# Other memory for the first ring slots, later loads of four heads' query weights, and 64x64 blocks for every weighted row

## The reference

```python
q = (ub @ wq).reshape(tb, PEER_HEADS, 2, PEER_DKEY // 2)
s1 = jnp.einsum('thd,hnd->thn', q[:, :, 0], sub_keys[:, 0])
s2 = jnp.einsum('thd,hnd->thn', q[:, :, 1], sub_keys[:, 1])
t1, i1 = lax.top_k(s1, PEER_TOPK)
t2, i2 = lax.top_k(s2, PEER_TOPK)
...
g = jax.nn.softmax(top.astype(jnp.float32), axis=-1)
act = jax.nn.gelu(jnp.einsum('td,tkd->tk', ub, up[eidx]))
return jnp.einsum('tk,tkd->td', g * act, down[eidx])
```

## Time and profile before

| | |
|---|---|
| median of 3 runs | 4134.78 us (4134.16 to 4145.85) |
| profiled execution, its own time | 4144.19 us |
| span of that execution (first to last instruction) | 4142.4 us |
| PE (TensorE matmul) busy | 3560.7 us, 86% |
| VectorE (DVE) busy | 2749.1 us, 66% |
| ScalarE (ACT) busy | 1717.3 us, 41% |
| GpSimd (POOL) busy | 1877.7 us, 45% |
| DMA queue of the gathers, share of 16 engines | 81.4% |
| mean granted clock of TensorE | 0.980 |

### The profile page before, as it was taken

How to read it: one execution, slowest core, us unless ns; L and a number is a source line. 1 busy time by engine, 2 the same in 40 slices (tenths; PEclk the granted TensorE clock), 3 DMA queues, 4 the chain that set the end, 5 groups by cost and what they waited for, 6 DMA issues and landing times.

```text
span 4142.4 us, 46906 instructions
## 1 busy us (share of the span) xinstructions
PE 3560.7 (86%) x12376; PEld 1549.9 (37%) x12376; DVE 2749.1 (66%) x6907; ACT 1717.3 (41%) x4832; POOL 1877.7 (45%) x1449
## 2 busy tenths in 40 slices
PE   6999999888888888887788877889988888888887
PEld 3445654433333333333211111665433333333332
DVE  3205677777767677777766765668767777767775
ACT  2013625444444444444444443454444444444443
POOL 1112116556556556554434432213545655655555
PEclk9998999999999999999999998999999999999999
DMA  7742349999999999999999998547999999999997
GB/s 278 243 174 57 130 186 416 421 421 421 420 419 415 415 420 416 415 418 416 416 418 409 412 415 322 146 183 293 421 421 421 421 419 416 420 413 415 414 421 331
DMA packets 244603, 1496.45 MB, mean 361 GB/s; under 512 B 25665, under 2 KB 44609, under 8 KB 73649
## 3 DMA queue, kind: packets, MB, share of 16 engines
q0 software_dynamic: 191232, 1385.58, 81.4%
q1 hardware_dynamic: 53168, 108.50, 7.6%
HBM read 1487.57 MB, written 2.21 MB: 360 GB/s over the span
## 4 chain that ended last, share of the span: by engine, by line
DMA 45%; PE 27%; issue 8%; DVE 7%; ACT 6%; POOL 5%; POOLq 0%; DVEq 0%; SPq 0%; ACTq 0%; PEldq 0%
DMA arena<-in_updown,arena 43%; PE psum L1197 8%; POOL arena L1798 4%; DVE arena L2312 4%; PE psum L1140 3%; PE psum L988 3%; PE psum L1004 2%; ACT arena L1585 1%; PE psum L1012 1%; PE psum L1167 1%; ACT arena L1581 1%; PE psum L1273 1%; ACT L1634 1%; ACT L1570 1%; PE psum L1095 1%
## 5 line engine op out<-in xcount | busy, mean ns | idle before, releaser
L1798 POOL DMA_INDIRECT arena<-in_updown,arena x1280 | 1755.4, 1371 | 1739.2 <-PE psum L1197 822.4
L1197 PE MATMUL psum<-arena 128*128 128x512 f32 x4096 | 1992.2, 615 | 340.5 <-ACT arena L1585 323.3
L2312 DVE CUSTOM_DVE_ANT_0 arena<-arena 128x1024 bf16<-128x1024 f32 x1276 | 1565.3, 1227 | 902.1 <-DMA arena<-in_updown,arena 795.9
L1197 PEld LDWEIGHTS psum<-arena 128*128 128x128 f32 x4096 | 710.7, 190 | 1393.9 <-ACT arena L1585 835.2
L1634 ACT ACTIVATE arena<-arena 128x1 f32<-128x1 f32 x1280 | 259.1, 202 | 1665.8 <-DVE arena L2312 1662.8
L1585 ACT ACTIVATE arena<-CN,arena 128x128 f32<-128x128 f32 x1280 | 513.9, 402 | 44.8
L1273 PE MATMUL psum<-arena 64*64 64x512 f32 x2048 | 290.4, 639 | 137.2 <-ACT arena L1585 137.0
L1581 ACT ACTIVATE arena<-arena 128x1 f32<-128x1 f32 x1280 | 376.7, 294 | 67.2 <-ACT arena L1634 4.3
L1167 PE MATMUL psum<-arena 128*128 128x256 f32 (+1 forms) x1280 | 363.1, 384 | 3.0 <-ACT arena L1556 1.6
L1167 PEld LDWEIGHTS psum<-arena 128*128 128x128 f32 x1280 | 239.0, 190 | 260.1 <-issue 252.3
L1273 PEld LDWEIGHTS psum<-arena 64*64 64x64 f32 x2048 | 54.5, 135 | 327.4 <-ACT arena L1585 313.2
(11 more groups left out here) (236 smaller groups left out, 2689.5 us busy)
## 6 DMA issues: line engine op xcount, KB each, us to landing
arena<-in_ada_w POOLq DMA_DIRECT2D x40, 1024.0 KB, 5.9
arena<-in_updown,arena POOLq DMA_INDIRECT x1280, 14.7
arena<-in_wq SPq DMA_DIRECT2D x16, 1024.0 KB, 18.9
arena<-in_w_in SPq DMA_DIRECT2D x50, 256.0 KB, 7.3
arena<-in_w_in SPq DMA_DIRECT2D x5, 2048.0 KB, 14.5
arena<-in_w_in SPq DMA_DIRECT2D x17, 512.0 KB, 4.8
arena<-in_ada_w SPq DMA_DIRECT2D x4, 2048.0 KB, 14.5
arena<-in_bias SPq DMA_DIRECT2D x16, 512.0 KB, 5.9
```

Source lines behind the costliest of these rows:

```text
L1197: mm = e.matmul(ps[ACCUMULATORS[t % 2][hf]][:], diag[:, k % DIAGS, :], ring[k % RING][:, D + hf * 512:D + (hf + 1) * 512], start=first, st ...
L1798: e.indirect_dma_start(ring[k % RING], None, updown, bass.IndirectOffsetOnAxis(ap=idx16[:, k:k + 1], axis=0)).then_inc(sem(f"rows{k % RING ...
L2312: e.tensor_tensor_reduce(prod[:, k % 2, :], ring[k % RING][:, 0:D], u, 1.0, 0.0, ALU.mult, ALU.add, dots[:, k:k + 1]).then_inc(sem("expert ...
```

## The change

It has three parts.

1. The first four gathers of each layer go to `early_ring`, the parts of `wk` that belong to heads 4 to 7, and wait for nothing but their indices. The ring's order is turned: slots 0 to 3 are now the four in `wo`, used from k = 8 on, and slots 4 to 6 the three in `mixT`.
2. The query weights of heads 4 to 7 may not be loaded before those four rows have been weighed: SP waits for `slot_done` 4 ahead of `load_head(4)`. The row `g2r`, issued behind the heads on the same queue, comes after them.
3. `weigh` has the body of `weigh_quarters` everywhere, and ScalarE always reads the swapped half with two instructions of 64 partitions.

```diff
-        ring = ([Region(mixer_top + n * 2 * D)(2 * D) for n in range(MIX_SLOTS)] + [Region(wo_at + n * 2 * D)(2 * D) for n in range(WO_SLOTS)]
+        ring = ([Region(wo_at + n * 2 * D)(2 * D) for n in range(WO_SLOTS)] + [Region(mixer_top + n * 2 * D)(2 * D) for n in range(MIX_SLOTS)]
                 + [last_slot])
+        LATE_HEADS = PH - WO_SLOTS
+        early_ring = [wk[:, 2 * (LATE_HEADS + n):2 * (LATE_HEADS + n) + 2].rearrange("p c k n -> p (c k n)") for n in range(WO_SLOTS)]
+
+        def slot_rows(n, k):
+
+            return early_ring[k] if isinstance(n, int) and n + k < WO_SLOTS else ring[k % RING]
...
                 for h in range(1, PH):
+                    if h == LATE_HEADS:
+                        e.wait_ge(sem("experts.slot_done"), WO_SLOTS)
                     load_head(h)
...
                     for hf in range(2):
-                        mm = e.matmul(ps[ACCUMULATORS[t % 2][hf]][:], diag[:, k % DIAGS, :], ring[k % RING][:, D + hf * 512:D + (hf + 1) * 512],
-                                      start=first, stop=last, skip_group_check=True)
+                        for i in range(2):
+                            rows, o = slice(64 * i, 64 * i + 64), 64 * (i ^ hf)
+                            mm = e.matmul(ps[ACCUMULATORS[t % 2][hf]][o:o + 64, :], diag[rows, k % DIAGS, rows],
+                                          rows_at[rows, D + hf * 512:D + (hf + 1) * 512], start=first, stop=last, skip_group_check=True)
...
-                    if k < MIX_SLOTS:
-                        turned = min(2 * (k + 1) - t0, nt)
+                    if WO_SLOTS <= k < WO_SLOTS + MIX_SLOTS:
+                        turned = min(2 * (k - WO_SLOTS + 1) - t0, nt)
                         if turned > 0:
                             e.wait_ge(sem("experts.y_ready"), turned)
-                    if k == MIX_SLOTS:
-                        e.wait_ge(sem("experts.y_ready"), nt)
                     if k == RING - 1:
                         e.wait_ge(sem("experts.ln1_done"), 1)
+                    if k == RING:
+                        e.wait_ge(sem("experts.y_ready"), nt)
```

More of the change, by code:

```diff
@@ L1195, in weigh @@
                     e.wait_ge(sem("experts.diag_ready"), n + (k + 1))
+                    if not isinstance(n, int):
+                        e.sem_inc(sem("pe_token"), 1)
+                    rows_at = slot_rows(n, k)
                     for hf in range(2):
-                        mm = e.matmul(ps[ACCUMULATORS[t % 2][hf]][:], diag[:, k % DIAGS, :], ring[k % RING][:, D + hf * 512:D + (hf + 1) * 512],
-                                      start=first, stop=last, skip_group_check=True)
+                        for i in range(2):
+                            rows, o = slice(64 * i, 64 * i + 64), 64 * (i ^ hf)
+                            mm = e.matmul(ps[ACCUMULATORS[t % 2][hf]][o:o + 64, :], diag[rows, k % DIAGS, rows],
+                                          rows_at[rows, D + hf * 512:D + (hf + 1) * 512], start=first, stop=last, skip_group_check=True)
                     mm.then_inc(sem("experts.slot_done"), 1)
@@ L1265, in section_mm @@
                         mm.then_inc(sem("ahead.slice_mm"), 1)
[L1267 to L1275, removed]
                 def ahead_unit(t, h):
@@ L1288, in ahead_unit @@
                             section_mm(x, y, a)
-                        (weigh_quarters if t >= CTX_AT else weigh)(t, un * TOPK, k, h == 0 and k == 0, h == PH - 1 and k == TOPK - 1)
+                        weigh(t, un * TOPK, k, h == 0 and k == 0, h == PH - 1 and k == TOPK - 1)
                 def folding_unit(h, turn=None):
@@ L1695, in tile @@
                     e.activation(ysb[:, 0:512], sums[0][:], ACT.Copy)
[L1696 to L1700, removed]
+                    e.activation(ysb[0:64, 512:D], sums[1][64:P, :], ACT.Copy)
+                    ins = e.activation(ysb[64:P, 512:D], sums[1][0:64, :], ACT.Copy)
                     ins.then_inc(sem("experts.acc_free"), 1)
@@ L1795, in _, with gather @@
                 meet(e, "pool")
-                def gather(k):
-                    e.indirect_dma_start(ring[k % RING], None, updown,
+                def gather(k, rows):
+                    e.indirect_dma_start(rows, None, updown,
                                          bass.IndirectOffsetOnAxis(ap=idx16[:, k:k + 1], axis=0)).then_inc(sem(f"rows{k % RING}"), 16)
@@ L1802, in _ @@
                         e.wait_ge(sem("experts.idx_ready"), k // RING + 1)
-                    if k < MIX_SLOTS:
-                        turned = min(2 * (k + 1) - t0, nt)
+                    if WO_SLOTS <= k < WO_SLOTS + MIX_SLOTS:
+                        turned = min(2 * (k - WO_SLOTS + 1) - t0, nt)
                         if turned > 0:
                             e.wait_ge(sem("experts.y_ready"), turned)
-                    if k == MIX_SLOTS:
-                        e.wait_ge(sem("experts.y_ready"), nt)
                     if k == RING - 1:
                         e.wait_ge(sem("experts.ln1_done"), 1)
+                    if k == RING:
+                        e.wait_ge(sem("experts.y_ready"), nt)
                     if k >= RING:
                         e.wait_ge(sem("experts.slot_done"), k + 1 - RING)
-                    gather(k)
+                    gather(k, slot_rows(0, k))
                 with e.Fori(1, nt * PH) as un:
@@ L1820, in _ @@
                         e.sem_inc(sem("pool_token"), 1)
-                        gather(k)
+                        gather(k, ring[k % RING])
         @block.vector
@@ L2311, in dot @@
                         e.wait_ge(sem("experts.dot_done"), un * TOPK + (k - 1))
-                        e.tensor_tensor_reduce(prod[:, k % 2, :], ring[k % RING][:, 0:D], u, 1.0, 0.0, ALU.mult, ALU.add, dots[:, k:k + 1]).then_inc(sem("experts.dot_done"), 1)
+                        e.tensor_tensor_reduce(prod[:, k % 2, :], slot_rows(un * TOPK, k)[:, 0:D], u, 1.0, 0.0, ALU.mult, ALU.add, dots[:, k:k + 1]).then_inc(sem("experts.dot_done"), 1)
                     def opening_unit():
```

2 lines of the change are left out of this document (1 added, 1 removed).

## The result

Over 16 runs each, the changed kernel takes 4154.7 us (median; 4147.3 to 4163.2) and the kernel before 4140.4 us (4131.2 to 4145.9): a ratio of 1.0039, 95% interval 1.0029 to 1.0049, or some 16 us (0.0039 x 4140; the interval is 12 to 20 us). The two medians themselves differ by 14.3 us. The profiled execution took 4158.8 us with a span of 4157.0, against a span of 4142.4 before: 14.6 us more.

What follows compares the result with a forecast made beforehand. The prediction took DMA transfers, at 421 GB/s in both expert stages, as the bound. Layer 0 (10.0 - 2.5), layer 1 (10.0 - 2.0) and the tail 0.5 summed to +16.0 us on 4134.8, giving 4150.8, range 4130 to 4162.

Steps and rivals of the forecast that it cites:

- The ceiling, 421 GB/s: In both expert stages transfers set the pace, at most 421 GB/s over long stretches, so one gather costs 2.49 us.
- Part 1, early gathers: Each layer's opening: four more gathers move early, 10.0 us of transfer, mostly spent as idle time before the eleventh gather.
- The eleventh gather 2.2 us sooner through quarters: Each opening: quarters shorten the chain to the third weighed row by 2.2 us, so this gather goes out at 611.5 and 2848.1.
- The stretch behind it stays full: After the eleventh gather until about 660 us in layer 0, likewise layer 1: losses avoided, gaining 2.5 and 2.0 us.
- Part 2, 10.0 us a layer: Query weights of heads 4 to 7, 4.19 MB, issued around 613 when the engines are full, cost 10.0 us per layer.
- Part 3 in the full stretches, nothing: Quarters in the full-size stretches: worth at most 14.6 us, taken as nothing because the DMA share is 1.01 in both.
- The tail, +0.5: After the last row, the second read of the sums becomes two of about 0.5 us each, adding 0.5 us.
- The sum: Whole kernel: (10.0 - 2.5) + (10.0 - 2.0) + 0.5 = +16.0 us, with chance 0.60.
- the +25: Full-size stretches: extra loss if 2420 us ran at the quarters stretch's 414 GB/s, 40 us instead of 14.6; not counted.
- the first (quarters win back 14.6): Full stretches: losses of 14.6 us come from late slots and quarters regain them, giving 4136.2 us; chance 0.20.
- the second (the lower clock binds): Slots with key scores at 1.2 GHz overrun, leaking 0.2 us in each of 64 units, +13, giving 4164 us; chance 0.10.
- The third rival (loads slip into gaps): Slots, not bytes, set the pace: late loads cost nothing and all losses are regained, -18.6, giving 4116 us; chance 0.10.

Runs made afterwards that it cites:

- e2: The changed kernel with full-size weighing and the sums' reading as before, so early gathers and late loads only; ratio 1.0076 to the kernel before.
- e1: The kernel before with every row weighed in quarters (64x64 blocks), its ring and loads unchanged; ratio 0.9998 to the kernel before.
- e3: The changed kernel with the query weights of heads 4 to 7 never loaded; ratio 0.9989 to the kernel before (4130.1 us).
- e5: The changed kernel with each late head's query weights loaded twice, its fold waiting for both; ratio 1.0087 to the kernel before.
- e4: The kernel before with quarters and the wait for four weighed rows before head 4's load, its own ring, no early gathers; ratio 1.0045 to the kernel before.
- e6: The changed kernel with two early gathers and two late heads (6 and 7, released by the second weighed row) instead of four; ratio 0.9996 to the kernel before.
- e7: The changed kernel with four rows weighed in the opening instead of two, ahead of head 2's fold; ratio 1.0016 to the kernel before.

## Why the prediction was right

4150.8 us was forecast and 4154.7 measured; the step was forecast at +16.0 and came out at a ratio of 1.0039, some 16 us. The forecast's base was the median of three runs, which lies 5.6 us below that of the 16 beside the changed kernel; from that base the forecast would have been 4156.4, so its miss of 3.9 us is one of the base more than of the step. That the step agrees to a fraction of a us is luck: the interval is 12 to 20 us, and by the gathers' starts the profiled execution lost some 18 us where the change acts. By its steps:

- *The ceiling, 421 GB/s.* Right. No long stretch of any of the ten kernels stands above it by more than 1, with one or two queues at work, at a granted clock of 0.85 (the changed kernel, 660 to 1100 us) or of 1.00 (e2, 650 to 1090 us). The 358 GB/s of the page cited in the prediction is not a limit here. Another page of the Trainium skill (HBM Reference, Specifications (TRN2)) says that a core streaming alone reaches about 425 GB/s and that 358 is its share when both cores of a pair stream; this kernel runs on one core, and the trace's 421 agrees with that.
- *Part 1, early gathers, worth nothing of their own.* Right in the main: the pairs put them at 0.6 to 2.7 us a layer of 10.0, and the share of 0.54 from 589.6 to 612.6 shows where 8.7 went.
- *The eleventh gather 2.2 us sooner through quarters.* Right in both layers (2.2), and shown to be part 3's doing: e1 has it at -2.2, e2 at 0.0. The empty engines start again some 2.2 us after its issue: the share is 0.19 until 612.6 and 0.94 from there.
- *The stretch behind it stays full.* Right: 420 GB/s to 660 us, where the earlier trace rows had 307 and 408. What it gives back was put too high: by e1's slot shifts -2.2 in layer 0 (forecast -2.5) and -0.9 in layer 1 (forecast -2.0), and at the last gathers only -1.0 and -0.9.
- *Part 2, 10.0 us a layer.* Right, and the main term. Three pairs price it: the changed kernel over e3 (11.6 and 10.9), e5 over the changed kernel (11.5 and 10.4), e4 over e1 (11.1 and 8.8). The first and the third hold 1.2 us of `g2r`; less that, the six lie between 7.6 and 11.5, with a mean of 9.9. The issue at about 613 came out at 612.2 to 613.8, and the wait of head 4 at nothing, as costed. The working behind that wait was off without harm: the loads did not get half of the rate but 35%, and the slowest took 31.1 us to land, not some 20.
- *Part 3 in the full stretches, nothing.* Right within 2 us: between the 101st and the last gather of layer 0 the kernels in quarters lie between -0.4 and +1.9 us of before, the changed kernel at +1.2.
- *The tail, +0.5.* It was +0.7 in the profiled execution.
- *The sum.* 7.5, 8.0 and 0.5 were forecast; by the gathers' starts they were 9.1, 8.2 and 0.7, less 3.4 us of scatter outside the two expert stages. Layer 0's excess is 0.5 us at the 101st gather and 1.2 us behind it. The prediction's 2420 us of full-size stretches fit no row; 64 units of 16 gathers at 2.49 us are 2550. It entered only the +25 that was set aside.

Of the rivals, e1 excludes the first (quarters win back 14.6) and the second (the lower clock binds): the clock was as low as feared, in 1.98 us rows, and a slot was freed in time all the same. The prediction gave that rival little because the clock returned within a few us whenever TensorE was fully busy; slices of 103.6 us can't show that, and in the kernel before TensorE was busy for 13.65 us of the 13.70 from 2673.3 us on with a granted clock of 0.50. The Trainium skill (TensorE: Matmul & The Clock Gate, Why this matters for your kernels) warns of gaps between bursts for the clock's sake; the trace agrees that the clock falls (0.72 from 640 to 660 us, with idle times of 1.8 to 2.8 us between the rows shown), and here it cost nothing, because the DMA engines stayed full all the while (share 1.01 or 1.02). The third rival (loads slip into gaps) is false for this kernel by e3 and e5. But e6 shows its condition: the same kind of load, issued at 601 instead of 612, does for the most part slip into a gap.

## What to carry to other kernels

When transfers set the pace, price a moved load by the state of the DMA engines at the moment it is released: here 2.1 MB released at 601 us, ahead of the last empty moment, cost 1 to 3.5 of their 5 us, and 4.2 MB released some 12 us later cost their full 10. Transfers brought forward are worth only what the next gap does not swallow, so find the first instruction after which the engines never stand empty (here the eleventh gather) and ask what makes that one earlier. And compare positions inside the program (the 101st gather from the first) when the total scatters by more than the effect.

## What the runs showed of the hardware

**The first mixer takes one of two courses.** The first gather of layer 0 stands at 548.1 to 549.3 us in five of the profiled executions and at 537.7 to 539.6 in four, with one at 543.3, though the edits touch nothing that runs before 440 us, and the two groups have parted by then. From the windows of three kernels, first before and e4 (first gather at 549.20 and 548.22), then e1 (539.62):

```profile
400.00:440.00 40.00, 30.84 (x147) 22.83 (x146) 26.53 (x112) 20.37 (x45) 14.84 (x17) 0.57 0.19 66
```

```profile
400.00:440.00 40.00, 30.89 (x152) 23.07 (x152) 27.05 (x113) 20.68 (x48) 15.46 (x18) 0.55 0.19 66
```

```profile
400.00:440.00 40.00, 28.69 (x221) 21.47 (x222) 32.00 (x125) 26.30 (x59) 20.57 (x25) 0.83 0.19 67
```

In 40 us the first two get through about 150 matmul records at a granted clock of 0.55 to 0.57, the third through 221 at 0.83. The changed kernel (0.55) belongs to the first kind and e2 (0.79), e5 (0.83) and e7 (0.87) to the second. The times of the kernel before form two groups as far apart: of its 16 runs beside the changed kernel, 7 lie between 4131 and 4137 us and 8 between 4141 and 4146. That they are the same two is likely but not shown, since one execution of it was profiled (4144.19 us, first gather at 549.20). What decides which course an execution takes was not tried. A comparison of a 10 us effect by three runs can be off by as much as the effect.

**A lower mean clock that cost nothing.** Quarters alone (e1) took the mean granted clock from 0.98 to 0.89 with transfers at the same 421 and 417 GB/s and a ratio of 0.9998. A weighed row took 1.09 us at the upper level and 1.98 at the lower, so TensorE's busy time stretches with the clock and doesn't tell what a row costs the kernel.

**Loads beside gathers.** From 612 to 644 us the changed kernel's loads (4.56 MB on q1, `g2r` included) and gathers (8.42 MB on q0) shared the engines at 35% and 65%, and the total was 420 GB/s from 616 us on, against 421 with gathers alone: the second queue took its share and added nothing.
